# Eighty-one U units as unsplit fp32 products, and 64 instead of 48 tokens by fetched rows, in a two-block transformer kernel

## What is computed

```python
qh = (xt @ w_peer_q).reshape(T, 8, 2, 128)
s = einsum('thpd,hpnd->thpn', qh, sub_keys)            # 8 heads, 2 halves, 128 keys
sv, si = top_k(s, 16)                                  # then the 16 best of 16 x 16 pairs
expert_idx = 128 * si[half 0] + si[half 1]             # 8 x 16 of 16384 experts per token
gates = softmax(best)
hval = einsum('cd,chkd->chk', x, expert_u[expert_idx])
out = einsum('chk,chkd->cd', gates * gelu(hval), expert_v[expert_idx])
```

## Time and profile before

| | us |
|---|---|
| Median of 3 timed runs | 1325.79 (1324.89 to 1327.82) |
| The profiled execution, its own time | 1323.25 |
| Its span, first to last instruction | 1321.3 |
| Ranking with 55 U units | 617 to 758 |
| Gates with 52 U units | 769 to 944 |
| 20 last U units and 20 V units | 944 to 1047 |
| 100 dense V units | 1047 to 1287 |
| End | 1287 to 1321.3 |

### The profile page before, as it was taken

The page is one execution under the profiler, slowest core; times in us unless marked ns, Lnnn a source line. Parts: engine busy times, 40 slices in busy tenths (PEclk is TensorE's granted clock), DMA queues, the critical chain, the costliest instruction groups (busy, mean ns, idle before and its releaser), DMA issues.

```text
span 1321.3 us, 21738 instructions
## 1 busy us (share of the span) xinstructions
PE 1298.0 (98%) x8066; PEld 1199.7 (91%) x8066; DVE 1067.7 (81%) x1964; ACT 818.5 (62%) x1601; POOL 215.6 (16%) x153
## 2 busy tenths in 40 slices
PE   8999999999999999999999989999999999999998
PEld 6998888888889888889999989999989999999995
DVE  6867776666777675778999779999988898999985
ACT  6886555555556555455677688888665555555553
POOL 3002030000000000000000010110233444654510
PEclk9999999999999999999999999999999999999999
DMA  6534366565535345654566755566688999999982
GB/s 228 179 122 136 112 225 191 189 186 190 184 131 174 128 144 176 223 197 144 192 215 201 231 199 200 202 209 209 235 291 311 353 383 351 356 377 363 356 275 93
DMA packets 83135, 292.73 MB, mean 222 GB/s; under 512 B 10749, under 2 KB 11405, under 8 KB 82774
## 3 DMA queue, kind: packets, MB, share of 16 engines
q1 hardware_dynamic: 68182, 239.65, 53.1%
q0 software_dynamic: 14848, 51.69, 11.0%
HBM read 288.95 MB, written 2.34 MB: 220 GB/s over the span
## 4 chain that ended last, share of the span: by engine, by line
PE 80%; DVE 9%; DMA 5%; ACT 4%; issue 2%; POOL 0%; SPq 0%; POOLq 0%; ACTq 0%; DVEq 0%
PE bank L2404 78%; DMA raw<-in_wts 4%; DVE wl L661 3%; DVE rows L1599 1%; ACT wh L1743 1%; PE bank L2502 1%; PE bank L2490 1%; DMA rows<-in_u_rows,pick 1%; DVE oi L1576 0%; ACT oi L2324 0%; DVE gates L1631 0%; DVE gates L1584 0%; DVE oj L1572 0%; ACT oi L2328 0%; DVE us L1590 0%
## 5 line engine op out<-in xcount | busy, mean ns | idle before, releaser
L2404 PE MATMUL bank<-hTb,wh 128*128 128x416 f32 (+3 forms) x2768 | 826.8, 363 | 5.4 <-DVE wl L661 3.8
L2404 PE MATMUL bank<-hTb,wl 128*128 128x208 f32 (+2 forms) x2584 | 651.9, 264 | 0.0
L661 DVE TENSOR_TENSOR wl<-raw,wh 128x1024 fp32r<-128x1024 f32 x429 | 522.4, 1224 | 134.5 <-ACT wh L1743 133.1
L1743 ACT ACTIVATE wh<-raw 128x1024 fp32r<-128x1024 f32 x429 | 449.4, 1056 | 207.7 <-PE bank L2404 113.9
L2404 PEld LDWEIGHTS bank<-hTb,wh 128*128 128x128 f32 (+1 forms) x2768 | 505.5, 188 | 28.7 <-issue 6.7
L2404 PEld LDWEIGHTS bank<-hTb,wl 128*128 128x128 f32 (+1 forms) x2584 | 492.0, 190 | 4.8
L2404 PE MATMUL bank<-wh,hTb 128*128 128x512 f32 (+2 forms) x552 | 175.0, 398 | 1.4 <-DVE hTb L695 1.4
L2404 PEld LDWEIGHTS bank<-wh,hTb 128*128 128x128 f32 (+1 forms) x552 | 102.1, 186 | 24.3 <-DVE wl L661 1.6
L641 POOL DMA_INDIRECT rows<-in_v_rows,pick x48 | 95.9, 1998 | 92.5 <-DVE acc L1610 80.7
L641 POOL DMA_INDIRECT rows<-in_u_rows,pick x48 | 71.5, 1489 | 235.9 <-DVE dots L1599 231.7
L2404 PE MATMUL bank<-wl,hTb 128*128 128x512 f32 (+2 forms) x276 | 100.3, 389 | 0.0
(11 more groups left out here) (429 smaller groups left out, 1403.0 us busy)
## 6 DMA issues: line engine op xcount, KB each, us to landing
raw<-in_wts SPq DMA_DIRECT2D x441, 512.0 KB, 4.3
x<-in_x SPq DMA_DIRECT2D x4, 256.0 KB, 6.9
sk<-in_sk SPq DMA_DIRECT2D x1, 1024.0 KB, 6.8
spill<-x SPq DMA_DIRECT2D x1, 1024.0 KB, 7.6
xr<-few_x POOLq DMA_DIRECT2D x2, 512.0 KB, 12.3
x<-spill SPq DMA_DIRECT2D x4, 256.0 KB, 7.4
rows<-in_u_rows,pick POOLq DMA_INDIRECT x48, 7.5
rows<-in_v_rows,pick POOLq DMA_INDIRECT x48, 8.2
```

Of the source, the lines that this page charges most:

```text
L661: e.tensor_tensor(b[:, :], raw[u % RAW][:, :], a[:, :].bitcast(F), ALU.subtract).then_inc(S("lo"), 1)
L1743: e.activation(parts_of(u)[0][:, :], raw[u % RAW][:, :], ACT.Copy).then_inc(S("hi"), 1)
L2404: return e.matmul(o, l, r, start=first, stop=last, skip_group_check=True)
```

## The change

The first `NP` units of the U pass fall from 55 to 32. The units with `whole(n)` (n < 81, all under the ranking and all beside the gates) are not split. TensorE multiplies `raw` itself, as fp32, with `xT`, an exact fp32 copy of the turned activations (`unit_W`); no `high`, no `low`, no `low_half`, no `ones` matmul. Such a `raw` buffer is free only when TensorE is done with the unit. `MORE` grows from 16 to 32, so 64 tokens fetch rows and 192 are dense: 128 fetches instead of 96, `TN` = 192, `NC` = 48, `GATED` = 81. 60 slots stand beside the gates (n = 36 to 80, one each and two where n is a multiple of 3), 19 beside the 47 split U units (81, 83, 85, 87, then every second from 99 to 127), 49 in the V pass. The GELU of the `dots` moves from the V pass to the U pass, three units after slot 63. `xT` costs ScalarE four copies (`rows_turned`) and TensorE three waits for them.

```diff
-NP, NB = 55, 5
-MORE = 16
+NP, NB = 32, 5
+MORE = 32
-SUMMED = NP + 1
-SOON = 16
+def whole(n):
+    return n <= NP or n < GATED
...
-        low_half = [sb("low_half0", [128, TN], FR, X0 + 5120), M("low_half1", [128, TN], FR)]
-        ones = M("ones", [128, 128], FR)
+        xT = M("xT", [128, 8, TN])
...
         def slots_taken():
-            at = {GATED - 1 - 3 * k: SOON - 1 - k for k in range(SOON)}
-            for n in range(GATED, NE - 2, 2):
-                at[n] = len(at)
-            left = 2 * SLOTS - len(at)
+            gates_at = [n for n in range(NP + 4, GATED) for _ in range(1 + (n % 3 == 0))]
+            late_at = [GATED + 2 * k + (10 if len(gates_at) + k >= SLOTS else 0) for k in range(19)]
+            left = 2 * SLOTS - len(gates_at) - len(late_at)
             last = DENSE - HOLD - 2
-            return at, {k * (last - 2) // (left - 1) + (2 if len(at) + k >= SLOTS else 0): len(at) + k for k in range(left)}
+            return gates_at + late_at, [2 + k * (last - 2) // (left - 1) for k in range(left)]
+        DOTS = (slots_taken()[0] + [NE + n for n in slots_taken()[1]])[SLOTS - 1]
...
             def weights(n):
                 for u in range(loaded[0], n):
-                    if u >= RAW:
-                        e.wait_ge(S("lo"), u - RAW + 1)
+                    if u >= RAW and as_whole(u - RAW):
+                        e.wait_ge(S("done"), u - RAW + 1)
+                    elif u >= RAW:
+                        e.wait_ge(S("lo"), nth_split(u - RAW))
...
+            def rows_turned(i):
+                q, j = i // 2, i % 2
+                e.wait_ge(S("hT_lo"), 20 + turned_at(5, i)[1] + 1)
+                copy(xT[:, 4 * j:4 * j + 4, 128 * q:128 * q + rows_of(q)],
+                     B[turned_at(5, i)[0]][:, :].rearrange("p (k t) -> p k t", k=4)[:, :, 0:rows_of(q)]).then_inc(S("hT_hi"), 1)
...
             turn_high(5, 3)
+            rows_turned(0)
             high(Q0 + 6)
+            rows_turned(2)
             queries_turned(0)
+            rows_turned(1)
             high(Q0 + 7)
             queries_out(1)
+            rows_turned(3)
...
             def block_out(n):
-                e.wait_ge(S("done"), nth("U", ORDER[n]) + 1)
-                if not added(n):
+                if not whole(n):
+                    e.wait_ge(S("done"), nth("U", ORDER[n]) + 1)
                     e.wait_ge(S("gelu"), n - 1)
-                copy((low_half if added(n) else us)[n % 2][:, :], B[2 + n % 4][:, TN:2 * TN]).then_inc(S("u_out"), 1)
+                    copy(us[n % 2][:, :], B[2 + n % 4][:, TN:2 * TN]).then_inc(S("u_out"), 1)
...
-            at_keys = {20: (0, 0, 0), 21: (0, 0, 1), 23: (0, 1, 0), 25: (0, 1, 1),
-                       36: (1, 0, 0), 37: (1, 0, 1), 38: (1, 1, 0), 39: (1, 1, 1)}
+            at_keys = {14: (0, 0, 0), 15: (0, 0, 1), 16: (0, 1, 0), 17: (0, 1, 1),
+                       22: (1, 0, 0), 23: (1, 0, 1), 24: (1, 1, 0), 25: (1, 1, 1)}
...
-                if n == 41:
+                if n == 26:
...
             for n in range(GATED, NE):
                 block_out(n)
                 gelu(n - 1)
+                if n == DOTS + 3:
+                    e.wait_ge(S("used"), used_by(SLOTS - 1))
+                    e.activation(factor[:, :], dots[:, :], ACT.Gelu).then_inc(S("used"), 1)
...
+            def unit_W(unit, o, width):
+                n = nth(*unit)
+                assert n == started[0], (unit, units[started[0]])
+                started[0] += 1
+                e.wait_ge(S(f"raw{n % RAW}"), 16 * (n // RAW + 1))
+                for k in range(8):
+                    t = mm(o, raw[n % RAW][:, two(128, k)], xT[:, k, 0:width], k == 0, k == 7)
+                t.then_inc(S("done"), 1)
...
             def early(n):
                 if n >= 4:
                     e.wait_ge(S("gelu"), n - 3)
-                unit_M(("U", ORDER[n]), B[2 + n % 4], width=TN)
-                if n and added(n - 1):
-                    e.wait_ge(S("u_out"), nth_out(n - 1))
-                    mm(B[2 + (n - 1) % 4][:, 0:TN], ones[:, :], low_half[(n - 1) % 2][:, :], False, True).then_inc(S("u_add"), 1)
+                if whole(n):
+                    unit_W(("U", ORDER[n]), B[2 + n % 4][:, 0:TN], TN)
+                else:
+                    unit_M(("U", ORDER[n]), B[2 + n % 4], width=TN)
```

More of the change, by code:

```diff
@@ L388, in nth_sum, with as_whole, nth_split @@
                 return n - 3
[L389 to L397, removed]
-        def nth_out(n):
-            return 13 + n
+            return nth_out(n)
+        def nth_out(n):
+            return 12 + sum(i >= NE or not whole(i) for i in range(n + 1))
+        def as_whole(u):
+            return units[u][0] == "U" and whole(u - nth("U", ORDER[0]))
+        def nth_split(u):
+            return sum(not as_whole(i) for i in range(u + 1))
         def of_expert(n):
@@ L652, in low @@
                 for u in range(lows[0], min(n + 1, len(units))):
-                    e.wait_ge(S("hi"), u + 1)
+                    if as_whole(u):
+                        continue
+                    e.wait_ge(S("hi"), nth_split(u))
                     if units[u][1] == "w_ple_gate":
@@ L1614, in vector, with slots_at @@
             at_u, at_v = slots_taken()
+            def slots_at(n):
+                for j, m in enumerate(at_u + [NE + v for v in at_v]):
+                    if m == n:
+                        slot_taken(j)
             for c in range(NB - 1):
@@ L1624, in vector @@
                 gated(n - 1)
-                if n in at_u:
-                    slot_taken(at_u[n])
+                slots_at(n)
                 v = B[(0, 1, 6, 7)[c % 4]][:, :].rearrange("p (t i) -> p i t", t=4)
@@ L1673, in vector @@
                 low(nth("D", "peer_expert_v_2", ORDER[n]) + LOOK)
-                if n in at_v:
-                    slot_taken(at_v[n])
+                slots_at(NE + n)
                 if n == DENSE:
@@ L2291, in keys_out @@
                 copy(key[a][:, s, :, :], bc(f4[:, s, a, :], 3, 16)).then_inc(S("key"), 1)
-            copy(ones[:, :], ident[:, :])
-            at_keys = {20: (0, 0, 0), 21: (0, 0, 1), 23: (0, 1, 0), 25: (0, 1, 1),
-                       36: (1, 0, 0), 37: (1, 0, 1), 38: (1, 1, 0), 39: (1, 1, 1)}
+            at_keys = {14: (0, 0, 0), 15: (0, 0, 1), 16: (0, 1, 0), 17: (0, 1, 1),
+                       22: (1, 0, 0), 23: (1, 0, 1), 24: (1, 1, 0), 25: (1, 1, 1)}
             for n in range(NP):
@@ L2343, in scalar @@
                 copy(gates[:, 0:NE - n, two(4, c)], v[:, 0:NE - n, :]).then_inc(S("G_out"), 1)
-            after_dots = {j: n for n, j in slots_taken()[1].items()}[SLOTS - 1] + 1
             def high_of(n):
@@ L2376, in scalar @@
                 high(nth("D", "peer_expert_v_2", ORDER[n]) + LOOK)
-                if n == after_dots:
-                    e.wait_ge(S("used"), used_by(SLOTS - 1))
-                    e.activation(factor[:, :], dots[:, :], ACT.Gelu).then_inc(S("used"), 1)
                 if n == DENSE:
@@ L3107, in tensor @@
                     e.wait_ge(S("u_sum"), nth_sum("w_peer_q_2", n - 4))
+                elif n == 5:
+                    e.wait_ge(S("hT_hi"), 27)
                 unit_M(("E", "w_peer_q_2", 128 * n), query_bank(n))
```

8 lines of the change are left out of this document (4 added, 4 removed).

## The result

The changed kernel takes **1356.18 us** (median, 1353.65 to 1360.17) against 1325.34 of the kernel before on the same chips: a ratio of 1.023, 95% interval 1.0204 to 1.0256. It is slower; the forecast was 1319, and the range ended at 1345. The profiled execution has a span of 1355.7.

The account below looks back on a forecast made before the run. TensorE, 98% busy, bounds the kernel, with row fetches tight beside the gates. First slots by 739, last gate slot 893, unit 84 at 897.4, V 1003.1 to 1280.1, span 1313.8: forecast 1319 us, range 1302 to 1345.

Parts of the forecast that it names:

- TensorE's prices: TensorE's cost per unit: 2.6 us unsplit at 192 columns, 2.30 split U or dense V, 3.48 per gate chunk.
- From `chosen` to the first row fetch POOL took 32.2 us ...; nothing in that changes but which tokens.: POOL's stretch after the choice, with the xr and pick copies, stays 32.2 us: first fetch at 728.5.
- the slot, 2.70: Beside the gates, three row buffers turn in 8.1 us (landing 6.4, use 1.2, wake 0.5): 2.70 us per slot.
- rival B: Beside the gates, rows land as slowly as in later stages: 1343 at 7.7, 1353 at 8.2; chance 0.25 with C.
- 4.5 for late weights and rows as in 944 to 1047: Behind the gates, 44 split U units take 101.2 us plus 4.5 of stalls, so V starts at 1003.1.
- The slot wait hides: At the turn, late weights stop TensorE some 3 us, covered by its wait for the first slots.
- The gap of 5 us at the turn that I let go: The 4.7 us stall at the turn to the gates goes, since ScalarE no longer waits for weights there.
- My sum to the first three slots: Up to the turn: first fetch 728.5, landing at 734.9, first three slots used by 739.
- Rival A: Beside the gates, fetches keep up (landing under about 6) and TensorE's 3.48 per chunk binds: 1305 us; chance 0.27.
- rival C: Units at 192 tokens still take 2.40 us, adding 16 us: 1335; counted inside B's chance, 0.25 together.

Follow-up runs that it names:

- rows4: The changed kernel with a fourth rows buffer for the 64 U slots, three in V as before: 1331.3 us.
- nolate: The changed kernel without fetches and VectorE's work for the 60 slots beside the gates and all but one of the 19 beside split U units: 1294.5 us.
- xr_sp: The changed kernel with both xr copies issued by SP between two units' weights instead of by POOL: 1339.7 us.
- sp_45: The changed kernel with both xr copies issued by SP and one slot per chunk beside the gates (45 instead of 60): 1326.2 us.
- early4_60_8: The changed kernel with an early first xr copy, the second in four SP pieces, a fourth U rows buffer, 8 slots beside split units: 1305.1 us, ratio 0.9864.

## Why the prediction was wrong

- **TensorE's prices** were right. Unsplit units took 2.6, a chunk 3.5, `chosen` 696.5, the first gate product 709.4. A unit at 192 tokens was forecast at 2.30: V took 276.9 for 277. That the sum agrees to 0.1 us is luck: a unit without a stall takes 2.28 and V's stalls 3.3 us, where 2.30 and 1 were taken. TensorE in order of time, after (start, us, instruction):

```profile
1045.76 0.25 PE L2424 MATMUL bank<-ab,wl 128*128 128x192 f32 x1
1045.85 0.36 PE L2424 MATMUL bank<-ab,wh 128*128 128x384 f32 x1
1046.05 0.25 PE L2424 MATMUL bank<-ab,wl 128*128 128x192 f32 x1
1046.13 0.36 PE L2424 MATMUL bank<-ab,wh 128*128 128x384 f32 x1
```

  The narrow one is 0.09 or 0.08 apart from the next, the wide 0.20, 0.28 a pair. The Trainium skill's rule for a weight load ("TensorE: Matmul & The Clock Gate", "LDWEIGHTS"), columns / 1.2, would be 107 ns; the start-to-start time of the narrow one is below that, so a narrow matmul has no floor of 107 ns. The trace doesn't contradict the load's own duration: a pair has two loads, 214 ns by that rule, in 0.28 us.
- **The failing step, first part: "From `chosen` to the first row fetch POOL took 32.2 us ...; nothing in that changes but which tokens."** It took 46.7. MORE went from 16 to 32, so few_picks grew from 48 to 64 tokens and the second copy from eight reads of 16 rows to four of 32. Before, POOL issued both copies at once and waited 16.75 us after them; now it waits after each. I had seen one wait of 16.75 in that stretch and carried it over as a constant, without asking what it was. POOL in order of time, before:

```profile
746.99 1.33 POOL L623 DMA_DIRECT2D xr<-few_x  x2 [2.60 <-DMA few_picks<-chosen]
765.07 0.75 POOL L623 DMA_DIRECT2D pick<-few_picks  x1 [16.75 <-issue]
```

  The first copy is the same in both kernels (32 rows, four times), and before, the second followed it at once. So the wait ahead of the second goes with what changed there: 400 packets of 4 bytes instead of 144 and, if the inference above holds, 32 rows one behind the other on an engine instead of 16. The few_picks copy had landed in both kernels before POOL went on. No run tried either size by itself, so what tips it is read from the traces, not shown.
- **Second part: the slot, 2.70.** That the turn of three buffers sets the pace was right, rows4 shows it. The landing was mis-sized: 6.4 taken, 7.1 in the mean by the sum's own terms, 5.6 to 8.7 on the chain. Three fetches always in flight beside weights are the conditions of V, where the row said 8.2, not of the gates. That is rival B's mechanism, priced at 1343 for 7.7; its point of decision, 6.8, was passed. It cost 57 x 0.24 = 14 us.
- **Third part: "4.5 for late weights and rows as in 944 to 1047".** From unit 84 to V it was 118.2 instead of 105.7. I had taken the stalls of a stage with 40.6 units over to 44 units. But that stage was 20 U units and 20 V units, and the trace before has 3.0 us of TensorE's idle time from 944 to 996, among the U units, and 0.7 from 996 to 1047: at 0.15 per U unit, 44 make 6.5. What stalls the rest are the slots, as nolate shows (14.8 us for 18 of them, 2.30 per unit without). That it is the shorter unit, 2.3 instead of 2.4, which leaves VectorE no room for them is argued, not tried.
- "The slot wait hides" a late weight at the turn: true in the changed kernel. In xr_sp the wait was gone and the weight stood there in its place.
- The gap of 5 us at the turn that I let go came back as 14.6 plus half clock. My sum to the first three slots was 739; they were used by 753.9.
- Sum of the parts: 14.9 to slot 2, 14 in the slots' pace, 0.7 from the last slot to unit 84 (5.2 for 4.5), 12.5 from there to V: 42 of 42. Rival A (the rows keep up) needed the fourth buffer and an early xr copy (the least landing in the earlier trace rows is 4.2, the 4.4 that it called the least is a median); rival C (no saving at 192 tokens) did not occur.

## What to carry to other kernels

When a change makes the bound engine faster, every chain that ran in its shadow has a new due time: list each with its slack before (here 13 us between the landing of the first fetch and the first slot) and subtract. An "issue" wait behind a DMA in the chain is a cost with a cause, not a constant: look at the number and size of its packets, and at how many are under way at once, before moving or resizing it. Where buffers turn in a ring, take the landing from a stretch with as many transfers in flight as the new schedule will have, and try one more buffer first: here 4 KB per partition gave 25 us.

## What the runs showed of the hardware

- A copy on POOL's queue that repeats its source rows through a broadcast dimension brought some 400 packets of 4 bytes for 128 rows, with at most four rows under way at a time, and took 14.6 to 16.0 us to land. In the changed kernel POOL stood 14 to 15 us behind each; in the kernel before it stood behind the pair only. As plain copies of the same rows it issued eight in 3.9 us.
- Reading 32 rows four times took 0.27 to 0.28 us per 4 KB packet, 128 different rows 0.18 (both beside weights); in the changed kernel the weights' packets beside it took 0.26.
- With both copies on SP's queue (sp_45) a weight issued 1 us behind them took 21.4 us to land.
- The granted clock was halved for 17.1 us from 738.7, 2.1 us into TensorE's wait of 14.6 for the late rows; in early4_60_8, without such a wait, it stays at 1.00 in all three stages.
